# Hyena long convolution: three index exchanges of each turn taken from TensorE and VectorE to DMA through DRAM

## The reference, cut to what matters

```
hy = dwconv1d(hy_in, ...)
v, x1, x2 = split(hy, 3)
k_f = hyena_filter_fft(L, ...)            # filter: small MLP -> taps * decay -> rfft over 2L
z = x1 * fft_long_conv(v, k_f[:, 0], bias[0])
z = x2 * fft_long_conv(z, k_f[:, 1], bias[1])
fft_long_conv(u, k, b) = irfft(rfft(u, 2L) * k)[:L] + u * b
```

## Time and profile before

| | |
|---|---|
| median of 3 runs | 3146.26 us (3144.06 to 3146.97) |
| profiled execution | 3143.5 us |
| its span, first to last instruction | 3141.7 us |
| PE busy | 2947.5 us, 94% of the span |
| DVE, ACT, POOL busy | 54%, 30%, 21% |
| granted clock of TensorE, mean | 0.970 |

### The profile page before, as it was taken

The page is one execution under the profiler, slowest core; times in us unless marked ns, Lnnn a source line. Parts: engine busy times, 40 slices in busy tenths (PEclk is TensorE's granted clock), DMA queues, the critical chain, the costliest instruction groups (busy, mean ns, idle before and its releaser), DMA issues. The chain is left out here.

```text
span 3141.7 us, 40466 instructions
## 1 busy us (share of the span) xinstructions
PE 2947.5 (94%) x16404; PEld 2547.7 (81%) x16404; DVE 1689.8 (54%) x1888; ACT 928.5 (30%) x1608; POOL 668.8 (21%) x344
## 2 busy tenths in 40 slices
PE   5999999979999998598899999999999999999998
PEld 3777887878888888577788888888888887788886
DVE  6664564556666666464575565565565563322223
ACT  5443434145545554355510100100100103211111
POOL 3133233102222221344132222222222210000000
PEclk7999999989999999799999999999999999999999
DMA  6111221422121211444411111111111105322222
GB/s 228 69 58 70 73 79 63 123 118 86 56 86 61 82 59 53 135 134 154 154 35 55 48 34 55 48 34 55 48 34 55 48 25 190 119 75 75 82 86 72
DMA packets 92739, 252.84 MB, mean 80 GB/s; under 512 B 14846, under 2 KB 53246, under 8 KB 83198
## 3 DMA queue, kind: packets, MB, share of 16 engines
q1 hardware_dynamic: 92608, 251.00, 23.5%
HBM read 175.01 MB, written 75.96 MB: 80 GB/s over the span
## 5 line engine op out<-in xcount | busy, mean ns | idle before, releaser
L1813 PE MATMUL out_up_banks<-xh_rest,up_w_hi 128*128 128x512 f32 (+2 forms) x1408 | 493.6, 351 | 9.4 <-DVE xl_rest L1923 7.3
L1813 PE MATMUL out_up_banks<-xh_rest,up_w_lo 128*128 128x512 f32 (+2 forms) x1408 | 493.7, 351 | 0.0
L1813 PE MATMUL out_up_banks<-xl_rest,up_w_hi 128*128 128x512 f32 (+2 forms) x1408 | 493.4, 350 | 0.0
L1969 DVE SCALAR_TENSOR_TENSOR ffn_hidden<-grid,params,ffn_hidden 128x2048 f32<-128x2048 f32 x176 | 457.7, 2601 | 24.6 <-DVE ffn_hidden L1966 0.2
L2125 PE MATMUL down_banks<-down_hi,down_h_hi 128*128 128x512 f32 x748 | 293.4, 392 | 11.3 <-DVE down_gate L2206 5.3
L1813 PEld LDWEIGHTS out_up_banks<-xh_rest,up_w_hi 128*128 128x128 f32 x1408 | 266.5, 189 | 40.9 <-DVE xl_rest L1923 8.1
L2125 PE MATMUL down_banks<-down_lo,down_h_hi 128*128 128x512 f32 x748 | 292.6, 391 | 0.0
L2125 PE MATMUL down_banks<-down_hi,down_h_lo 128*128 128x512 f32 x748 | 292.5, 391 | 0.0
L1813 PEld LDWEIGHTS out_up_banks<-xl_rest,up_w_hi 128*128 128x128 f32 x1408 | 266.3, 189 | 30.7
L136 POOL TENSOR_TENSOR up_w_hi<-up_w_whole,zero 128x1024 fp32r<-128x1024 f32 x44 | 124.2, 2822 | 779.9 <-PE out_up_banks L1813 763.3
L1813 PEld LDWEIGHTS out_up_banks<-xh_rest,up_w_lo 128*128 128x128 f32 x1408 | 266.3, 189 | 28.3
(11 more groups left out here) (267 smaller groups left out, 5773.3 us busy)
## 6 DMA issues: line engine op xcount, KB each, us to landing
hidden_ff_dram<-ffn_hidden SPq DMA_DIRECT2D x22, 1088.0 KB, 4.8
up_w_whole<-w_up_in SPq DMA_DIRECT2D x44, 512.0 KB, 5.2
pre_dram<-in_result SPq DMA_DIRECT2D x16, 1088.0 KB, 4.0
down_h<-hidden_ff_dram SPq DMA_DIRECT2D x88, 192.0 KB, 2.3
wada_late<-w_ada_late_in SPq DMA_DIRECT2D x32, 512.0 KB, 3.7
down_x<-w_down_in SPq DMA_DIRECT2D x22, 512.0 KB, 3.7
in_w_whole<-w_in_in SPq DMA_DIRECT2D x20, 512.0 KB, 4.5
home<-x_rows_in SPq DMA_DIRECT2D x17, 512.0 KB, 6.7
```

The lines of the kernel that those rows point to most:

```text
L1813: last = pe.matmul(out, weight[:, u, k], in_block(value, rest, b, k), start=(k == 0 and j == 0), stop=(k == KM - 1 and j == 2))
L1969: last = nc.vector.scalar_tensor_tensor(out=y, in0=window, scalar=weight, in1=y, op0=ALU.mult, op1=ALU.add)
```

## The change

All three exchanges go through DRAM. ACT evicts a batch of `first`, `f_first` or `back1` into one of four slots (`sent`, `f_sent`), SP sends the slot (256 KB, 2 KB from each partition) to a scratch tensor, and once that has landed SP fetches it (256 KB in 512-byte runs, to 16 partitions that lie 8 apart) into `spectrum`, `pairs` or `f_spectrum`. `turn_back`, `turn_pairs` and `f_turn_back` are gone from PE and DVE. In `first`, `f_first` and `back1` the table is now the stationary operand and the data the moving one, so that `first` and `f_first` are one matmul of 512 columns for a batch in place of two of 256 or four of 128. The tables are permuted to fit.

The turn's order is written in phases in place of the alternation: all of `turn_rows` and `first`; most of the filter's first half; `second` with `back1`; six `f_second`; `back2`; two `f_second`. SP now walks the same list as the engines. In it a fetch of batch j-2 stands behind the send of batch j. The loads of `gates` and the store of `z` stand at the head of a turn, the load of `v` or of the filter's inputs behind the last fetch of `back1`. The modulation tiles are requested by ACT, after it has evicted `ada`.

```diff
+def moved(stages, *names):
+    out = []
+    for stage, j in stages:
+        out.append((stage, j))
+        if stage in names:
+            out.append((stage + "_send", j))
+            if j >= 2:
+                out.append((stage + "_fetch", j - 2))
+            if j == 7:
+                out += [(stage + "_fetch", 6), (stage + "_fetch", 7)]
+    return out
...
+CONV_FIRST = (numbered("turn_rows", 0, 1) + numbered("first", 0, 1) + numbered("turn_rows", 2) + numbered("first", 2, 3)
+              + numbered("turn_rows", 3) + numbered("first", 4, 5, 6, 7))
+CONV_MIDDLE = (numbered("second", 0, 1, 2, 3) + [x for j in range(4) for x in (("back1", j), ("second", j + 4))]
+               + numbered("back1", 4, 5, 6, 7))
+CONV_LAST = numbered("back2", 0, 1, 2, 3)
+FILTER_FIRST, FILTER_SECOND = one_ahead("taps", "f_first"), numbered("f_second", *range(8))
...
+MOVED = ("first", "f_first", "back1")
+IN_GAP = 13
+CTX_FORWARD = [("ctx_turn", 0), ("ctx_taps", 0), ("ctx_forward", 0)]
+SEND_FIRST = moved([("bulk_first", 0)] + CONV_FIRST, *MOVED)
+FILTER_ONCE = moved(interleave(FILTER_FIRST, [("ctx_taps", 0), ("load_v", 0)]) + [("load_second", 0)], *MOVED)
+WITH_FILTER = (CONV_MIDDLE[:2] + FILTER_FIRST[IN_GAP:IN_GAP + 1] + CONV_MIDDLE[2:3] + FILTER_FIRST[IN_GAP + 1:IN_GAP + 2]
+               + CONV_MIDDLE[3:4] + FILTER_FIRST[IN_GAP + 2:] + interleave(CONV_MIDDLE[4:], ada(1) + ada(2)))
+BOTH = moved(interleave(FILTER_FIRST[:IN_GAP], CTX_FORWARD + ada(0)) + WITH_FILTER + [("bulk_last", 0)]
+             + interleave(FILTER_SECOND[:6], ada(3) + [("ctx_back", 0)]) + CONV_LAST
+             + interleave(FILTER_SECOND[6:], [("ctx_filter", 0)]), *MOVED)
+ONLY_CONV = moved([("ctx_turn", 0), ("ctx_forward", 0)] + ada(0) + ada(1) + CONV_MIDDLE + ada(2)
+                  + interleave(CONV_LAST, ada(3) + [("ctx_back", 0)]), *MOVED)
...
+def across(rows):
+    return rows.rearrange("(k s) i c -> (s i) k c", s=4)
...
+            for stage, j in FILTER_ONCE:
+                batch(stage, j, 0, 0, None, 0)
+            for stage, j in SEND_FIRST + [("load_tables", 0)]:
+                batch(stage, j, 0, 0, 0, 1)
+            for stage, j in FILTER_SECOND + [("ctx_filter", 0)]:
+                batch(stage, j, 0, 0, None, 0)
+            for turn in range(2 * CT):
+                ct, order = divmod(turn, 2)
+                for stage, j in (SEND_FIRST if turn else []) + (BOTH if turn < 2 * CT - 1 else ONLY_CONV):
+                    batch(stage, j, ct, order, turn, turn + 1)
...
+                    if stage in ("first_send", "back1_send"):
+                        stage = stage[:-5]
+                        sp.wait_ge(out[stage], turn * 8 + j + 1)
+                        sp.dma_start(d["swap_" + stage][j], sent[:, j % 4]).then_inc(sent_done[j % 4], 16)
...
+                    elif stage == "first_fetch":
+                        sp.wait_ge(sent_done[j % 4], sends_before("first", j, turn, f_turn) * 16 + 16)
+                        sp.dma_start(spectrum[SLOT_ROWS[j]:P:8], across(d["swap_first"][j])).then_inc(spectrum_loaded, 16)
...
+                    elif stage == "bulk_first" and turn:
+                        wait_for_turn(turn - 1)
+                        if order == 0:
+                            store_z(ct - 1)
+                        load_gates(ct, order)
+                    elif stage == "bulk_last" and ct + 1 < CT:
+                        if order == 1:
+                            load_v(ct + 1)
+                        else:
+                            ...
+                            load_filter_inputs(ct + 1)
...
-                        for q in range(2):
-                            last = pe.matmul(bank[:, 256 * q:256 * q + 256], rows[:, 2 * j + q], first_t[:],
-                                             start=True, stop=True)
-                    elif stage == "turn_back":
-                        ...
-                            last = pe.transpose(four(bank)[:, q], spectrum_c[:, 2 * g:2 * g + 2, :]
-                                                .rearrange("p r b -> p (r b)"), ident[:])
+                        last = pe.matmul(bank, first_t[:, j % 2], rows[:, j // 2 * 4:j // 2 * 4 + 4]
+                                         .rearrange("p s c -> p (s c)"), start=True, stop=True)
+                    elif stage == "second":
+                        if j == 0:
+                            pe.wait_ge(spectrum_loaded, turn * 128 + 128)
...
+                    elif stage == "back2":
                         if j == 0:
-                            pe.wait_ge(out["back1"], turn * 8 + 8)
+                            pe.wait_ge(pairs_loaded, turn * 128 + 128)
...
+                        if sends_before(stage, j, turn, f_turn):
+                            act.wait_ge(sent_done[j % 4], sends_before(stage, j, turn, f_turn) * 16)
+                        nc.scalar.activation(sent[:, j % 4].rearrange("p q c -> p (q c)"), bank,
+                                             ACT.Copy).then_inc(out[stage], 1)
...
+                        c = LATE_PER_TURN * turn + j + 2
+                        if c < LATE_TILES:
+                            nc.scalar.dma_start(wada[:, c % 2], d["w_ada_late"][c]).then_inc(ada_loaded[c % 2], 16)
```

More of the change, by code:

```diff
@@ L901, in interleave @@
     return [lists[n][i] for _, n, i in sorted(keyed)]
-CONV_FORWARD = ([("turn_rows", j) for j in range(4)] + [("first", j) for j in range(8)]
-                + [("turn_back", j) for j in range(8)] + [("second", j) for j in range(8)])
-CONV_BACK = ([("back1", j) for j in range(8)] + [("turn_pairs", j) for j in range(8)]
-             + [("back2", j) for j in range(4)])
+def moved(stages, *names):
[9 more added lines that the diff above has]
+    return out
@@ L911, in one_ahead, with numbered @@
 def one_ahead(producer, consumer):
     return [(producer, 0)] + [x for j in range(8) for x in ((producer, j + 1), (consumer, j)) if x[1] < 8]
-FILTER_FIRST, FILTER_SECOND = one_ahead("taps", "f_first"), one_ahead("f_turn_back", "f_second")
-CTX_FORWARD = [("ctx_turn", 0), ("ctx_forward", 0)]
-CTX_BACK = [("ctx_back", 0)]
-CTX_TAPS, CTX_FILTER = [("ctx_taps", 0)], [("ctx_filter", 0)]
-ADA = [(stage, j) for j in range(LATE_PER_TURN) for stage in ("ada", "ada_turn")]
-BATCHES = {"turn_rows": 4, "first": 8, "turn_back": 8, "second": 8, "back1": 8, "turn_pairs": 8, "back2": 4,
-           "taps": 8, "f_first": 8, "f_turn_back": 8, "f_second": 8,
+def numbered(stage, *which):
+    return [(stage, j) for j in which]
@@ L923 @@
+FILTER_CHAIN = FILTER_FIRST + FILTER_SECOND
+BATCHES = {"turn_rows": 4, "first": 8, "second": 8, "back1": 8, "back2": 4, "taps": 8, "f_first": 8, "f_second": 8,
            "ctx_turn": 1, "ctx_forward": 1, "ctx_back": 1, "ctx_taps": 1, "ctx_filter": 1,
            "ada": LATE_PER_TURN, "ada_turn": LATE_PER_TURN}
-ONLY_FILTER = FILTER_FIRST[:8] + CTX_TAPS + FILTER_FIRST[8:] + FILTER_SECOND + CTX_FILTER
-ONLY_CONV = interleave(CONV_FORWARD, CTX_FORWARD) + interleave(CONV_BACK, ADA + CTX_BACK)
-def merge(pattern, conv, filter_, ctx):
-    conv_left, filter_left = iter(conv), iter(filter_)
-    merged = [next(conv_left if x == "c" else filter_left) for x in pattern]
-    assert len(merged) == len(conv) + len(filter_)
-    return interleave(merged, ctx)
@@ L1102, in batch @@
                         if j == 0:
-                            pe.wait_ge(out["first"], turn * 8 + 8)
+                            pe.wait_ge(spectrum_loaded, turn * 128 + 128)
                         for q in range(4):
                             g = 4 * j + q
-                            last = pe.transpose(four(bank)[:, q], spectrum_c[:, 2 * g:2 * g + 2, :]
-                                                .rearrange("p r b -> p (r b)"), ident[:])
-                    elif stage == "second":
-                        pe.wait_ge(out["turn_back"], turn * 8 + j + 1)
+                            last = pe.matmul(four(bank)[:, q], second_t[:, g], spectrum[:, g], start=True, stop=True)
+                    elif stage == "back1":
+                        pe.wait_ge(slots_ready, turn * 8 + j + 1)
+                        if turn == 0 and j == 0:
+                            pe.wait_ge(tables_loaded, 16 * 4)
@@ L1219, in batch @@
                         act.wait_ge(mm[stage], turn * 4 + j + 1)
+                        if j == 2:
+                            act.wait_ge(out["back2"], turn * 4 + 4)
                         nc.scalar.activation(rows[:, 4 * j:4 * j + 4].rearrange("p q c -> p (q c)"), bank,
```

231 lines of the change are left out of this document (102 added, 129 removed).

## The result

The changed kernel takes 3210.35 us (median of 4 runs, 3206.85 to 3215.02) where the kernel before takes 3145.86: a ratio of 1.0209, 95% interval 1.0197 to 1.0221. It is 64 us slower; 3047 was forecast, with 3020 to 3100 as the range. The profiled execution took 3209.9 us.

The account below looks back on a forecast made before the run. PE's work was taken to bound the kernel. Phases summed to 61.0 us, 62 with 1 added, 14 less a turn; 18 at the start + 6 x 14 - 3 = 99 us less, giving 3047 us, range 3020 to 3100.

Parts of the forecast that it names:

- the cover of `back1`'s exchange: After the last `back1` batch, eviction, send and fetch take 6.8 us, hidden behind 8.4 us of six `f_second`.
- D: Turn phase of six `f_second` without transposes between them: 8.4 us, of which PE works 6.5.
- It fits, barely: Claim that DMA engines carry the exchanges: 53 to 59 us of their work in a turn of 61.
- L: Landing time of an exchange transfer, issue to landing: 2.5 us taken for a send, 2.7 for a fetch.
- The third rival: A fetch runs at half rate, 1.3 us for 1.0; a turn takes 64, total 3061 us; chance 0.10.
- the clock: PE's granted clock falls to 0.50 after pauses; two such pauses in the last turn, 0 to 8 us, 2 taken.
- A and B: Turn's opening: `turn_rows` and `first` 9.0 us, then `taps`, `f_first`, context and one `ada` 14.0 us.
- C: Turn phase of `second`, `back1`, rest of the filter's first half, two `ada`: 18.9 to 21.2 us, 20 taken.
- Start: Up to turn 1: it starts at 734.5 in place of 752.5, 18 us less; `v` about 1.4 us late.
- Last turn: Final turn, with no filter to cover the exchanges: 61 us for 60 before, plus 2 for clock; 3 more.
- The second: Exchanges land late, PE stands before `second` 0 and `back2` 0: 3076 us at L = 4.0, 3098 at 4.5; chance 0.27.
- The fourth: SP's single queue: fetches wait for sends, holding later sends; slower than before, 3160 us at L = 6.3; chance 0.11.

Follow-up runs that it names:

- e5_no_tiles: The changed kernel without the loads of 30 of the 32 modulation tiles: 3145.17 us, ratio 1.0002.
- e2_half: The changed kernel with half of every send and half of the `back1` and `f_first` fetches left out from turn 1 on: 3110.83 us.
- e1_fill: The changed kernel with added 512-column matmuls, results overwritten, where PE paused: 3160.05 us, ratio 1.0042.
- f1_filter_dma: The kernel before with only the filter's exchange by DMA; `f_second`, tile requests and bulk loads also moved: 3146.02 us.
- g1_pairs_pe: The changed kernel with `back1`'s exchange on PE transposes again, the other two by DMA: 3119.93 us, ratio 0.9918.
- h1_probe: The changed kernel with 256 KB transfers of six forms added at the idle end of the block: 3316.55 us, one run.
- e3_plain: The changed kernel with each fetch in 2 KB runs to all 128 partitions, index not exchanged: 3147.78 us.

## Why the prediction was wrong

**The step that failed** is the cover of `back1`'s exchange: "eviction 0.8, send 0.4 + 2.5, fetch 0.4 + 2.7 = 6.8 us, against D's 8.4". It took 15.5 us. The eviction took 2.9, because ACT first waited 2.84 for a slot, a wait that the forecast had priced for `first` and not here; the send and the fetch took 5.2 and 5.4 (medians). "It fits, barely" let the landings pass: the forecast took L from the 192 KB transfers of another block, and asked only for the mean of a turn. Alone, a fetch lands after 3.3 us, and back to back it holds the DMA engines 1.47 us, not 1.0. The mean load in a turn came out just above the forecast's (61 us for 53 to 59), but the traffic is bunched: a share of 0.97 in D, where the exchange meets the tiles and the filter's last fetches, and 1.04 in B. e5_no_tiles and e2_half show that fewer bytes there bring the landings down and the time with them. The third rival priced a fetch nearer (1.3 us), but it let DMA set only the length of the turn.

**The second mis-sized term is the clock.** The prediction charged it in the last turn only, with 2 us, although showed what a pause does. Pauses came into all turns, once the exchange was longer than D. Sized by the runs, of the 19.5 us by which a turn exceeds 62: at least 7.3 are clock (after to e1_fill), 9.0 are transfers that remain at full clock (74.2 to e2_half's 65.25; there the matmuls added in e1_fill are inside too, so a part of the 9.0 may belong to the clock), and 3.2 are left at half the bytes, spread over all phases (24.3, 21.4, 9.3 and 9.8 for 23, 20, 8.4 and 9.6, and 1 us forecast on top).

**Point by point.** A and B, 23 us: right (23.9). C, 20: 21.4 in e2_half, 24.0 after. In turn 2 PE stands 3.0 us there before an `f_first`; ACT waits 4.3 us for slots of `f_sent`, PE's weight load 3.2 us for that eviction, and the clock over C is 0.93. So slots are a part of C as well; how much was not measured. ACT's 21.9 us of waits for `swap_back` sends lie mostly at the head of D (five of 2.5 to 4.1 us). D, 8.4: right for PE and DVE (9.3 in e2_half), wrong as a cover for the exchange. `back2` and the rest, 9.6: right at full clock (9.8), 18.1 at half. Cost of a request by ACT, 0 to 0.4: 0.33 us each. What the tiles cost is their load (65 us by e5, which drops bytes and requests), which the forecast had only counted into the 17 to 25%; asking for them on SP's queue gave 22 us.

**Start**, forecast 18 us early, measured 18 late. The waits of PE there, on the timeline:

```profile
661.77 1.97 PE L1132 MATMUL conv_bank<-ident,hy_v 128*128 128x128 f32 x8 [4.98 <-DMA hy_v<-pre_dram]
...
675.54 2.92 PE L1175 MATMUL filter_bank<-f_spectrum,second_table 128*128 128x128 f32 x24 [1.81 <-DMA second_table<-second_table_in]
684.42 6.94 PE L1175 MATMUL filter_bank<-f_spectrum,second_table 128*128 128x128 f32 x40 [5.97 <-DVEq L1379]
697.67 2.04 PE L1212 MATMUL ctx_bank<-ctx_taps,ctx_forward_table 128*128 128x128 f32 x8 [6.31 <-DMA back_table<-back_table_in]
```

B began at 699.5 in place of 682.5: `v` 5 us late for 1.4, and 6.3 us for `back_table`, which SP's list issues behind all sends of A and which the forecast did not name. The other 18.7 us are turn 0's own B to F (70.7 for 52). That a different order of these loads would win them back was not tried.

**Last turn**, 63 forecast, 78.5 measured to the first matmul of the next block, 60.9 before (1208.83 to 1269.69). Timeline of PE:

```profile
1285.69 5.45 PE L1144 MATMUL conv_bank<-hy_spectrum,second_table 128*128 128x128 f32 x32 [8.58 <-DMA hy_spectrum<-swap_first_dram]
...
1314.73 3.65 PE L1156 MATMUL conv_bank<-back_table,hy_pairs 128*128 128x64 f32 x16 [7.47 <-DMA hy_pairs<-swap_back_dram]
```

Both waits were forecast; `second` starts 26.5 us after the turn and not 18, and `back2` runs at 3.65 us a batch behind its wait.

**The rivals.** The second (L = 4.0 to 4.5, 3076 to 3098) saw the places: PE stood before `back2` in every turn, 36.0 us in 8 waits, and before `second` only in 2 (11.1 us). Its formula for `second`, 8.7 + 4L, counts the last fetch twice: the working above it (3.0, three landings, 3, the last fetch) is 6.0 + 4L. For L = 4.5 that is 24 us against 23, and so PE seldom stood there. For `back2`, 1.9 + 2L at L = 5.3 is 4.1 us over D's 8.4, and the measured wait in turns 0 to 6 is (36.0 - 7.5)/7 = 4.1. The turn grew by 19.5, so most of it is not in that rival's sum. The fourth, slower by SP's queue alone from L = 6.0, did not come to pass: no median landing of an exchange reached 6.0. The kernel became slower by the second's mechanism at a longer landing, and by the clock that falls behind it. The chance given to slower was too small because L and clock were priced as if apart: what made PE wait here also halved the speed of what followed.

**How much of the gain was real.** With e2_half the turn is 10.8 us below that of before: the transposes' time was there to win, at half the bytes. f1_filter_dma won 0.5 us a turn in the old order with one exchange; g1_pairs_pe won 5 in the phases with two.

Open: how the 9.0 us a turn of e1_fill to e2_half split between waits and the matmuls added, how much of C is slots, and how much of D is ACT's wait for a slot. More slots were not tried, nor an order in which ACT evicts `f_second` ahead of `back1` 7.

## What to carry to other kernels

Add up what the DMA engines must carry in a turn at the rate of the very pattern used, and compare that with the turn it is to be hidden in; in phases whose DMA share was 0.9 to 1.04, landings were 4.0 to 5.4 us here, against 2.0 and 3.3 alone. Before an exchange goes from TensorE to DMA, ask what PE will do while it lands: idle time there can be paid a second time in the clock of the work behind it, so transposes that fill such a gap can be worth more than they cost. Taking work from a busy engine pays only if nothing else in the order holds it: in f1_filter_dma 16.6 us of work went, the wait for `taps` stayed and another grew. And look for a slot wait behind each pause: an engine that waits for one keeps back everything that stands behind it in its list (2.84 us of ACT, 5.10 of DVE).

## What the runs showed of the hardware

- 256 KB to 16 partitions: 178 GB/s when they lie 8 apart, 190 at 4 apart, 104 when adjacent, 279 in the same 512-byte runs to 128 partitions, 383 for a 2 KB send (h1_probe). The DMA share reads 1.24 to 1.29 in the slow forms, so a share near 1 is not yet full there.
- After two pauses of 1.0 and 1.3 us TensorE's granted clock went from 1.00 to 0.50, and 13.4 us of `back2` with PE busy throughout did not bring it back: it was 0.50 from 907.5 to 933.5 us and rose in the last microsecond of the turn. In e1_fill the same matmuls ran at full clock.
- The length of one pause does not tell whether the clock falls. In e5_no_tiles the pauses in D are the same in all of turns 1 to 6 (0.88, 0.33, 0.62 us); with a pause before `back2` of 1.33 and 0.82 us `back2` ran at full clock (7.33 us), with 0.84, 1.52, 1.76 and 1.88 it took 11.6 to 13.3.
- Executions of the versions on the edge of a pause scatter: e5_no_tiles from 3126.8 to 3154.6 and e3_plain from 3138.4 to 3167.1, where the kernel before stays within 3139.9 to 3147.0.
